# A hybrid attention and RWKV-7 encoder: how the triangular solver gets its first inverse, on which engine, and what stands around it

## What is computed

```
xs = tuple(jnp.moveaxis(t, 1, 0) for t in (r, decay, k, v, -kk, kk * a))
def step(state, inp):
    r_t, w_t, k_t, v_t, a_t, b_t = inp
    sa = jnp.einsum('bhvk,bhk->bhv', state, a_t)
    state = state * w_t[:, :, None, :] + sa[..., None] * b_t[:, :, None, :] + v_t[..., None] * k_t[:, :, None, :]
    return state, jnp.einsum('bhvk,bhk->bhv', state, r_t)
```

## Time and profile before

| | |
|---|---|
| median of 3 runs | 1164.71 us (1164.21 to 1165.63) |
| the profiled execution, its own time | 1167.3 us |
| its span, first to last instruction | 1165.3 us |
| PE busy | 1141.8 us |
| DVE busy | 795.8 us |
| ACT busy | 565.7 us |
| POOL busy | 2.1 us, 11 instructions |
| mean granted clock of the matrix engine | 0.993 |

### The profile page before, as it was taken

How to read it: one execution, slowest core, us unless ns; L and a number is a source line. 1 busy time by engine, 2 the same in 40 slices (tenths; PEclk the granted TensorE clock), 3 DMA queues, 4 the chain that set the end, 5 groups by cost and what they waited for, 6 DMA issues and landing times.

```text
span 1165.3 us, 27242 instructions
## 1 busy us (share of the span) xinstructions
PE 1141.8 (98%) x10716; PEld 1058.9 (91%) x10716; DVE 795.8 (68%) x1464; ACT 565.7 (49%) x1005; POOL 2.1 (0%) x11
## 2 busy tenths in 40 slices
PE   7999999999999999999999999999999999999998
PEld 6999999999978899999989999989999788999997
DVE  4666666889746866666686666677885568666665
ACT  4444444586234544444454444456843445444443
POOL 0000000000000000000000000000000000000000
PEclk8999999999999999999999999999999989999999
DMA  6666665754000466666556666666530014666663
GB/s 190 193 185 181 187 190 163 186 143 138 4 2 15 135 195 184 188 186 181 179 165 186 187 185 182 187 166 164 146 93 4 3 55 141 198 184 182 187 188 126
DMA packets 243958, 173.45 MB, mean 149 GB/s; under 512 B 14428, under 2 KB 228596, under 8 KB 243892
## 3 DMA queue, kind: packets, MB, share of 16 engines
q1 hardware_dynamic: 243892, 172.50, 50.8%
HBM read 171.43 MB, written 1.05 MB: 148 GB/s over the span
## 4 chain that ended last, share of the span: by engine, by line
PE 84%; DVE 9%; ACT 4%; issue 1%; DMA 1%; SPq 0%; ACTq 0%; DVEq 0%
PE bank L1361 24%; PE bank L1362 23%; PE bank L1363 23%; PE bank L1374 9%; DVE wlo L820 2%; DVE xlo L849 1%; PE bank L1368 1%; ACT whi L531 1%; DMA raw<-in_ffn_w_gate_dram 1%; PE bank L1500 1%; ACT work L646 1%; PE bank L1499 0%; DVE work L989 0%; PE bank L1675 0%; ACT xhi L547 0%
## 5 line engine op out<-in xcount | busy, mean ns | idle before, releaser
L820 DVE TENSOR_TENSOR wlo<-raw,whi 128x1024 fp32r<-128x1024 f32 (+1 forms) x322 | 392.7, 1221 | 242.6 <-ACT whi L531 242.1
L1361 PE MATMUL bank<-xhi,whi 128*128 128x256 f32 x1696 | 484.5, 286 | 6.7 <-DVE xlo L849 5.9
L1362 PE MATMUL bank<-xlo,whi 128*128 128x256 f32 x1696 | 480.6, 283 | 0.0
L1363 PE MATMUL bank<-xhi,wlo 128*128 128x256 f32 x1696 | 480.5, 283 | 0.0
L531 ACT ACTIVATE whi<-raw 128x1024 fp32r<-128x1024 f32 (+1 forms) x322 | 339.4, 1055 | 286.8 <-PE bank L1363 261.6
L1361 PEld LDWEIGHTS bank<-xhi,whi 128*128 128x128 f32 x1696 | 325.7, 192 | 13.8 <-issue 8.5
L1362 PEld LDWEIGHTS bank<-xlo,whi 128*128 128x128 f32 x1696 | 325.9, 192 | 3.7 <-issue 0.5
L1363 PEld LDWEIGHTS bank<-xhi,wlo 128*128 128x128 f32 x1696 | 325.8, 192 | 0.0
L1361 PE MATMUL bank<-whi,hhi 128*128 128x512 f32 x352 | 138.7, 394 | 1.2 <-DVE hlo L935 1.0
L1362 PE MATMUL bank<-wlo,hhi 128*128 128x512 f32 x352 | 138.0, 392 | 0.0
L1363 PE MATMUL bank<-whi,hlo 128*128 128x512 f32 x352 | 137.0, 389 | 0.0
(11 more groups left out here) (220 smaller groups left out, 1025.6 us busy)
## 6 DMA issues: line engine op xcount, KB each, us to landing
raw<-in_ffn_w_gate_dram SPq DMA_DIRECT2D x88, 512.0 KB, 3.9
raw<-in_ffn_w_up_dram SPq DMA_DIRECT2D x88, 512.0 KB, 3.9
raw<-in_ffn_w_down_dram SPq DMA_DIRECT2D x88, 512.0 KB, 3.5
raw<-in_w_in_dram SPq DMA_DIRECT2D x32, 512.0 KB, 3.9
raw<-in_w_out_dram SPq DMA_DIRECT2D x16, 512.0 KB, 3.9
raw<-in_w_q_up_dram SPq DMA_DIRECT2D x4, 384.0 KB, 3.3
xtok<-in_x_dram SPq DMA_DIRECT2D x4, 256.0 KB, 5.8
raw<-in_w_in_dram SPq DMA_DIRECT2D x4, 256.0 KB, 4.2
```

The source lines that it names most:

```text
L820: V_.tensor_tensor(wlo[:, b.slot, 0:width], raw[:, b.slot, 0:width], whi[:, b.slot, 0:width].bitcast(F32), ALU.subtract).then_inc(lo_ready, 1)
L1361: mm(out, hi, mhi, start=start, stop=False, **kw)
L1362: mm(out, hi, mlo, start=False, stop=False, **kw)
L1363: return mm(out, lo, mhi, start=False, stop=stop, **kw)
```

## The change

The Gram block is now masked and given its identity when it leaves the bank: DVE writes `M1` itself (strictly upper mask, then identity added in place, steps `m1a` and `m1`), and ACT's two copies are gone. GpSimd multiplies `M1` by `level1T`, which now holds the diagonal, and writes `pC`; `ti` waits for it through the semaphore `first_inverse`. The level masks hold the diagonal too. So the identity is in every factor, `t` and `p` are whole results of each level, all their products open and close their bank, and the two `tp` matmuls are gone. In the lists three things move: `r_c` behind `t0` on DVE, the split of block 23 and `sh_g0` behind `um1` on DVE, and the fill `tb` ahead of `u1` on PE with its two ACT copies ahead of `gs0`.

```diff
-        lev.append((row // (2 * s) == col // (2 * s)) & (row // s > col // s))
+        lev.append((row // (2 * s) == col // (2 * s)) & (row // s > col // s) | (row == col))
...
-    put("level1T", (row // 2 == col // 2) & (row < col))
+    put("level1T", (row // 2 == col // 2) & (row <= col))
...
+            for l in range(DEPTH):
+                for b in range(2):
+                    pool.wait_ge(mix_dve.sem, mix_dve.at(l, f"m1_{b}"))
+                    pool.tensor_tensor(pC[:, 8 * b:8 * b + 8, :], M1[:, 8 * b:8 * b + 8, 0, :],
+                                       con("level1T").unsqueeze(1).to_broadcast((P, 8, C)),
+                                       ALU.mult).then_inc(first_inverse, 1)
...
-                for b in range(2):
-                    act.wait_ge(mix_pe.sem, mix_pe.at(l, f"gb{b}"))
-                    nc.scalar.activation(M1[:, 8 * b:8 * b + 8, 0, :], bank[4 + b][:].rearrange("p (g i) -> p g i", g=8),
-                                         ACT.Copy).then_inc(mix_act.sem, mix_act.step(f"m1_{b}"))
                 squares("qsq", 0, H, 2 * H, True)
...
                 kept_tokens("tb", b_tok)
+                act.wait_ge(mix_dve.sem, mix_dve.at(l, "sh_g0"))
+                nc.scalar.activation(lora[:, 1, :], lora[:, 1, :], ACT.Tanh, scale=0.5)
+                nc.scalar.activation(lora[64:96, 2, :], lora[64:96, 2, :], ACT.Tanh,
+                                     scale=0.5).then_inc(mix_act.sem, mix_act.step("gs0"))
                 kept_tokens("tv", v_tok)
...
                 for b in range(2):
-                    dve.wait_ge(mix_act.sem, mix_act.at(l, f"m1_{b}"))
-                    V_.tensor_tensor(eight(pC, b), bank8(4 + b), con("level1T").unsqueeze(1).to_broadcast((P, 8, C)),
-                                     ALU.mult).then_inc(mix_dve.sem, mix_dve.step(f"p1a{b}"))
+                    dve.wait_ge(mix_pe.sem, mix_pe.at(l, f"gb{b}"))
+                    V_.tensor_tensor(M1[:, 8 * b:8 * b + 8, 0, :], bank8(4 + b), upper[:, 0:1, :].to_broadcast((P, 8, C)),
+                                     ALU.mult).then_inc(mix_dve.sem, mix_dve.step(f"m1a{b}"))
                 for b in range(2):
-                    dve.wait_ge(mix_dve.sem, mix_dve.at(l, f"p1a{b}"))
-                    V_.tensor_tensor(eight(pC, b), eight(pC, b), con("eyes").unsqueeze(1).to_broadcast((P, 8, C)),
-                                     ALU.add).then_inc(mix_dve.sem, mix_dve.step(f"p1_{b}"))
+                    m1 = M1[:, 8 * b:8 * b + 8, 0, :]
+                    dve.wait_ge(mix_dve.sem, mix_dve.at(l, f"m1a{b}"))
+                    V_.tensor_tensor(m1, m1, eyes, ALU.add).then_inc(mix_dve.sem, mix_dve.step(f"m1_{b}"))
...
                 tile("v1"), tile("v2"), tile("v3")
-                for b in range(2):
-                    pe.wait_ge(mix_dve.sem, mix_dve.at(l, f"p1_{b}"))
-                    pe.wait_ge(mix_dve.sem, mix_dve.at(l, f"pr_v{1 + b}"))
-                    ins = mm(bank[2 + b][:], ident, pC[:, 8 * b:8 * b + 8, :].rearrange("p g i -> p (g i)"),
-                             start=True, stop=False, skip_group_check=True)
-                    ins.then_inc(mix_pe.sem, mix_pe.step(f"tp{b}"))
                 tile("g0")
                 eyes = con("eyes")
                 for b in range(2):
+                    pe.wait_ge(first_inverse, 2 * l + b + 1)
                     pe.wait_ge(mix_dve.sem, mix_dve.at(l, ("pr_v3", "pr_g0")[b]))
```

More of the change, by code:

```diff
@@ L222 @@
          + tile_steps("r0", "kkms", *newton("kk"), "kkw", "lc") + tile_steps("r1", "kk", "kk2", "a_c", "b_c") + tile_steps("r2")
-         + tile_steps("r3") + tile_steps("v0", "p1a0", "p1a1", "p1_0", "p1_1") + tile_steps("v1")
-         + tile_steps("v2", "kmod") + tile_steps("v3", "r_c") + ["pr_g0", "t0_0", "t0_1", "sh_g0"]
-         + pair("um1") + ["kss", "qkms"] + newton("qk") + ["rqs", "k_c", "tc1_0"] + pair("br") + ["tc1_1"]
+         + tile_steps("r3") + tile_steps("v0", "m1a0", "m1a1", "m1_0", "m1_1") + tile_steps("v1")
+         + tile_steps("v2", "kmod") + tile_steps("v3") + ["pr_g0", "t0_0", "t0_1", "r_c"]
+         + pair("um1") + ["sh_g0"] + ["kss", "qkms"] + newton("qk") + ["rqs", "k_c", "tc1_0"] + pair("br") + ["tc1_1"]
          + pair("um2") + ["kn", "kx", "tc2_0"] + pair("gk") + ["tc2_1", "qg"]
@@ L235 @@
                    "mu_k3", "lw", "kksq", "kv_e", "mu_r0", "ksq0", "qe0", "qe1", "E", "einv", "mu_r1", "ksq", "qsq0",
-                   "mu_r2", "mu_r3", "kf", "mu_v0", "m1_0", "m1_1", "qsq", "mu_v1", "mu_v2", "mu_v3", "mu_g0", "gs0"]
-         + pair("tb") + pair("tv") + pair("pc1") + pair("tk") + pair("pc2") + pair("pc3")
+                   "mu_r2", "mu_r3", "kf", "mu_v0", "qsq", "mu_v1", "mu_v2", "mu_v3", "mu_g0"]
+         + pair("tb") + ["gs0"] + pair("tv") + pair("pc1") + pair("tk") + pair("pc2") + pair("pc3")
          + pair("Q0") + pair("Q1") + pair("pc4") + pair("Q2") + pair("Q3") + pair("pc5")
@@ L368, in build @@
         h_steps = sem("h_steps")
-        once = sem("once")
+        once, first_inverse = sem("once"), sem("first_inverse")
         x_turned, out_done = sem("x_turned"), sem("out_done")
@@ L707, in mixing @@
                 ahead(23), mu("g0")
[L708 to L711, removed]
                 def kept_p(k):
@@ L1119, in mixing @@
                 scale("v3"), ahead(22), mixed_with_last("v3")
-                per_chunk(lambda c: V_.tensor_tensor(grouped(AR[:, :, 1, :])[:, c], chunked(rT)[:, c],
-                                                     E_c[:, c, :, 1:C + 1],
-                                                     ALU.mult)).then_inc(mix_dve.sem, mix_dve.step("r_c"))
                 scale("g0")
@@ L1126, in mixing @@
                     V_.tensor_copy(eight(tC, b), bank8(b)).then_inc(mix_dve.sem, mix_dve.step(f"t0_{b}"))
-                ahead(23), mixed_with_last("g0")
-                upper = con("upper").rearrange("p (s i) -> p s i", s=2)
+                per_chunk(lambda c: V_.tensor_tensor(grouped(AR[:, :, 1, :])[:, c], chunked(rT)[:, c],
+                                                     E_c[:, c, :, 1:C + 1],
+                                                     ALU.mult)).then_inc(mix_dve.sem, mix_dve.step("r_c"))
                 def masked_u(k):
@@ L1150, in mixing @@
                 masked_u(1)
+                ahead(23), mixed_with_last("g0")
                 dve.wait_ge(mix_act.sem, mix_act.at(l, "qsq"))
@@ L1635, in fill @@
                         ins.then_inc(mix_pe.sem, mix_pe.step(f"{name}_{b}"))
+                fill("tb")
                 for k in LV:
@@ L1662, in mixing @@
                             g = 8 * b + j
-                            ins = both(bank[2 + b][:, 64 * j:64 * (j + 1)], uC[:, g, :], pC[:, g, :], False, last,
-                                       skip_group_check=True)
+                            ins = both(bank[2 + b][:, 64 * j:64 * (j + 1)], uC[:, g, :], pC[:, g, :], True, True)
                         ins.then_inc(mix_pe.sem, mix_pe.step(f"p{k}_{b}"))
```

15 lines of the change are left out of this document (5 added, 10 removed).

## The result

| | before | changed |
|---|---|---|
| median | 1165.2 us (1164.21 to 1166.22, 10 runs) | 1167.94 us (1166.48 to 1173.85, 10 runs) |
| profiled execution, span | 1165.3 us | 1165.8 us |
| mean granted clock of that execution | 0.993 | 0.994 |

The ratio is 1.003, with a 95% interval of 1.0017 to 1.0044: the change makes the kernel slower. The forecast was 1166.6 us with +1.9 us. The time lies inside the range, and on the far side of the 0.2% that I had called the same, which had been given a chance of 0.65.

A forecast was written before the change was run, and what follows sets the result against it. Matrix engine bound on average, but the vector engine sets the pace up to `ti_1`. Per layer -1.34 - 0.18 + 0.60 = -0.92, plus 1.86 for GpSimd, +0.94; two layers +1.9 on 1164.7 give 1166.6 us, range 1162.4 to 1168.2.

The forecast's parts named there:

- the 0.2% that I had called the same: Whole kernel: 1162.4 to 1167.0 us, within about 2.3 us, counts as no change; chance 0.65.
- `tp` gains nothing: Matrix engine ahead of `ti_1`: removing two `tp` saves 1.71 us, but none comes through, since `ti_1` still waits for `pr_g0`.
- `r_c` and ACT's copies: Vector engine ahead of `ti_1`: moving `r_c` gains 1.34 us and dropping ACT's copies 0.18 us a layer.
- GpSimd and the vector engine exclude each other: Ahead of `pr_g0`: instructions reading two SBUF operands wait for each other, GpSimd's product taking 1.06 us; chance 0.50.
- d: Delay of the vector engine ahead of `pr_g0` from GpSimd's two products, all paid by `ti_1`: 1.86 us a layer.
- The push of 0.80 us for the split: Vector engine: the split due at 275.41 is pushed by 0.80 us by GpSimd's first product.
- the 1.06 for the mixing: Vector engine: GpSimd's second product, if it gets in ahead of the next L989, pushes that by 1.06 us.
- The consequence in the sum: Start of `ti_1`: 1.34 and 0.18 us earlier by the moves, 1.86 us later by GpSimd; net 0.34 us later.
- The order behind `ti_1`: From `ti_1` to the end of `u2`: the moved split gives back 0.60 us a layer, `u2_1` waiting some 0.5 us.
- I work out one layer and double it: Both layers' solvers: the second repeats the first, so +0.94 us a layer becomes +1.9 us for the kernel.

The follow-up runs named there:

- the repeat: The changed kernel once more, its text differing only by an empty line; 1167.24 us, ratio 1.0029 against the kernel before.
- the pair with and without zeros: The changed kernel with the vector engine's old order, 1172.15 us; the same with zero products in the waits ahead of `ti_0` and `ti_1`, 1167.75 us.
- the filled kernels: The changed kernel with seven zero products ahead of `ti_0` and three ahead of `ti_1`, in two kernels alike; 1165.78 and 1166.68 us.

## Why the prediction was wrong, and what it had right

**`tp` gains nothing: right.** The L1585 rows are gone, g0 follows v3 (0.24 us late, since it waits for a stretched split), and `ti` still waits for `scale`.

**`r_c` and ACT's copies: right in size.** 1.44 us with a GpSimd that only writes, against 1.52.

**GpSimd and the vector engine exclude each other: right, and d = 1.81 us against 1.86.** The forecast placed d as gaps between the rows; it shows as longer rows. The push of 0.80 us for the split is 0.78, and the 1.06 for the mixing is 1.03. L820 and L989 are stretched by products and not by memsets, and L982, with one operand in PSUM, is not stretched by either (0.42 us). The Trainium skill, in SBUF — State Buffer, section Who interferes with whom, has a vector instruction with two SBUF inputs contend with a GpSimd instruction that reads SBUF, and not with one that only writes. The rows of both layers agree. The consequence in the sum, `ti_1` 0.34 us later, was 0.37.

**The order behind `ti_1`: right in kind.** The end of `u2` moved by +0.89 us against a forecast of +0.94, and the scores by +0.73 and +0.93 in the profile without stalls. Two layers are 1.65 us against +1.9. `u2_1` waits 0.18 us for `tc1_1` (0.33 in the repeat), where I expected 0.5.

**The step that failed is "I work out one layer and double it".** The sum carried the delay of one layer to both and put anything else that could hold the matrix engine behind `ti_1` at nothing. In the two profiles of the change the first layer loses 0.72 and 0.70 us, near the forecast's 0.94. The second loses 2.38 and 1.77, of which 1.62 and 0.96 us are the stalls marked "issue", a term that the sum didn't have. Both profiled executions lie near their medians (1167.60 and 1167.16 us, against 1167.94 and 1167.24), and the clock is at 1.00 through both solvers in each. Their marks add up to 3.10 and 2.47 us, which is enough for the 2.74 and 1.95 us between the medians. So 1.65 us of the loss is the forecast's mechanism, and the rest of about 1 us is, in the executions that a trace shows, these stalls. Why they come stays open. The one profile of the kernel before has none, but they are also there without GpSimd and without the new algorithm (0.99 us with the product on the vector engine, 1.10 us in the old algorithm with `r_c` moved).

**A second term was missing: what waits on the matrix engine do to its clock.** It waited 0.86 us ahead of `ti_1` and now waits 1.72 + 0.71 = 2.43 us a layer. That such waits can cost more than their length is shown by the pair with and without zeros. For the change itself it is argued and not shown. The same waits had the clock at 0.61 behind them in one profile (`tb` behind `u1`) and at 1.00 in the two of the change. Over all executions its mean clock is 0.9931, against 0.9944 of 99 executions of the kernel before; five of its 22 are at 0.991 or below against one of 99, and four took over 1170 us against none. So a low clock goes with the slow tail, which the means contain; the two profiles near the median show none in the solvers. Filling the waits took back 1.4 us of 2.2 to 2.7, not separate from none, and not by the clock as far as the executions tell: at the same mean clock of 0.994, eleven of the change have a median of 1167.3 us and nine of the filled kernels 1165.8. How the rest divides between stalls and clock over all executions stays open.

**The chances.** With +1.9 us I stood 0.4 us inside the boundary of 0.2% and gave 0.65 to "the same". The measured loss is 0.24% of the medians. The side was right, and so was the case, exclusion as in the forecast. The first layer's loss doubled, 1.4 us, would have stayed inside; it was the surplus of the second layer that moved the result across the line. That the time lies only 1.3 us from the forecast is in part luck: `ti_1` and `u2` were sized right, but the stalls could as well have been absent (1165.34 us in the profiled execution of the filled kernel that has none).

**What stays open.** The stalls marked "issue" come and go in the dense part of the solver, 0 to 1.6 us in a layer. I first held that they belonged to `tb` ahead of `u1`. That falls: they are there with `tb` behind it. The same instructions have them in one profile and not in the other, but where they come they often stand at the same product: ahead of the last 30 of one row in the change, its repeat and the kernel with the product on the vector engine. What holds the engine there no view shows.

## What to carry to other kernels

Before a piece is moved to GpSimd to relieve a vector engine without gaps, count what both read from SBUF: here each 128 by 512 product of two SBUF operands took 0.9 us from the vector engine, which does it itself in 0.6. And when an instruction is moved, list who queues behind each waiter on the other engines: the same move of `r_c` gained nothing with the tanh ahead of the `tb` copies, and 2.6 to 4.3 us with it behind them. Waits of the matrix engine ahead of dense work are worth filling with products of zeros where they reach 1.72 and 2.06 us as here; at 1.72 and 0.71 us the gain was not separate from none. And before one layer is doubled, look at the second one's own rows after the change.

## What the runs showed of the hardware

A conflict between GpSimd and the vector engine appears as a longer duration of the vector instruction (1.21 to 1.99 us, 0.48 to 1.51 us), not as idle time, so a view of waits doesn't show it. GpSimd's pair reads 3.90 us where the vector engine lost 1.8 us, so the length of its rows is not their price; how long a product takes with nothing beside it no run shows. The granted clock was at half (0.50 over 286 to 290 us) behind waits of 1.72 and 2.06 us on the matrix engine, 0.72 over 280 to 290 us, and stayed at 1.00 when products of zeros filled them. In one profile it fell behind waits of 1.73 and 0.71 us too (0.61 over 284 to 288 us). It also fell in the thin stretch behind the solver in most profiles, of the kernel before too (0.83 over 920 to 940 us); the kernel before has a median of 1163.05 us in its 17 executions at a mean clock of 0.997 and of 1165.98 in its 34 at 0.993, so the clock goes with much of the spread between executions. Rows of 64 by 64 products can also stand still for 0.2 to 1.2 us with nothing to wait for, in some executions and not in others.
